# Transformer decode step on one core: output projection and second norm by token halves, sums of squares with tokens on partitions

## The reference

```
h    = rms_norm(x, norm_mix) * (1 + sc1) + sh1
q, k, v, u = split(h @ w_in)
attn = MoBA attention(q, k, v)       # sample: scores over all cached keys, top 3 blocks, cached values
pool = multi-scale pooling(u)
x    = x + g1 * (concat(attn, pool) @ w_out)             # output projection
h    = rms_norm(x, norm_mlp) * (1 + sc2) + sh2           # second norm
x    = x + g2 * (square(relu(h @ w_up)) @ w_down)        # MLP
y    = rms_norm(x, norm_final)
```

## Time and profile before

| | |
|---|---|
| runs (median, low, high) | 1012.74, 1011.08, 1019.36 us |
| profiled execution | 1017.83 us |
| its span, first to last instruction | 1014.6 us |
| TensorE busy | 912.3 us, 90% |
| VectorE busy | 538.7 us, 53% |
| ScalarE busy | 225.9 us, 22% |
| GpSimd busy | 150.2 us, 15% |
| granted TensorE clock, mean | 0.942 |

### The profile page before, as it was taken

The page is one execution under the profiler, slowest core; times in us unless marked ns, Lnnn a source line. Parts: engine busy times, 40 slices in busy tenths (PEclk is TensorE's granted clock), DMA queues, the critical chain, the costliest instruction groups (busy, mean ns, idle before and its releaser), DMA issues.

```text
span 1014.6 us, 16468 instructions
## 1 busy us (share of the span) xinstructions
PE 912.3 (90%) x6421; PEld 590.7 (58%) x6421; DVE 538.7 (53%) x936; ACT 225.9 (22%) x372; POOL 150.2 (15%) x150
## 2 busy tenths in 40 slices
PE   4939999999988997399989989999899999999896
PEld 3417777555544433266666657666666666676554
DVE  5374321478776375956647756756746422442124
ACT  3123220433321012112032131220220221313102
POOL 0040750000000000511011020120110110301100
PEclk9759999799999999599999999999999899999898
DMA  9710226778858787588788888888975977559992
GB/s 295 286 50 1 84 84 221 282 233 278 273 185 283 275 285 284 196 289 292 258 334 290 275 301 304 272 301 292 328 266 176 364 234 239 168 193 381 385 385 100
DMA packets 133183, 254.21 MB, mean 251 GB/s; under 512 B 10454, under 2 KB 61387, under 8 KB 124907
## 3 DMA queue, kind: packets, MB, share of 16 engines
q1 hardware_dynamic: 95475, 183.54, 51.6%
q10 hardware_dynamic: 36864, 67.13, 19.4%
q0 software_dynamic: 768, 2.51, 0.6%
HBM read 248.57 MB, written 4.75 MB: 250 GB/s over the span
## 4 chain that ended last, share of the span: by engine, by line
PE 68%; DVE 13%; DMA 8%; ACT 4%; ACTq 3%; issue 3%; POOL 1%; SPq 1%; DVEq 0%; POOLq 0%
PE PS L1407 65%; DVE KT L1043 4%; DMA W<-in_w_up_dram 3%; ACTq L805 3%; DMA VR<-in_w_up_dram 2%; DVE hT L987 1%; DVE hT L986 1%; ACT W_split L768 1%; DMA smp<-in_x_sample_dram 1%; PE PS L1582 1%; DVE W_split L1194 1%; DMA VR<-in_cache_v_dram 1%; PE PS L1421 1%; DMA KR<-in_cache_k_dram 1%; PE PS L1955 0%
## 5 line engine op out<-in xcount | busy, mean ns | idle before, releaser
L1407 PE MATMUL PS<-H_split,W_split 128*128 128x512 f32 x672 | 236.4, 414 | 14.9 <-DVE W_split L1016 14.9
L1407 PE MATMUL PS<-gT_split,W_split 128*128 128x512 f32 x512 | 172.8, 402 | 3.0 <-POOL kT_split L653 3.0
L1407 PEld LDWEIGHTS PS<-H_split,W_split 128*128 128x128 f32 x672 | 132.1, 197 | 68.2 <-issue 23.9
L1043 DVE STREAM_TRANSPOSE KT<-KR 128x512 f32<-128x512 f32 x256 | 161.5, 680 | 18.9 <-DMA KR<-in_cache_k_dram 18.9
L1407 PE MATMUL PS<-hT_split,W_split 128*128 128x512 f32 x320 | 129.8, 406 | 0.0
L1194 DVE TENSOR_TENSOR W_split<-W,W_split 128x1024 fp32r<-128x1024 f32 x64 | 82.0, 1285 | 86.8 <-ACT W_split L768 86.8
L1407 PEld LDWEIGHTS PS<-gT_split,W_split 128*128 128x128 f32 x512 | 96.1, 188 | 49.7 <-issue 18.7
L768 ACT ACTIVATE W_split<-W 128x1024 fp32r<-128x1024 f32 x64 | 67.2, 1051 | 237.6 <-DMA W<-in_w_up_dram 136.4
L1407 PE MATMUL PS<-KT,qcur 128*32 128x128 f32 (+1 forms) x2080 | 76.0, 288 | 38.8 <-DVE KT L1043 34.6
L1407 PE MATMUL PS<-kT_split,W_split 128*128 128x512 f32 x256 | 100.3, 392 | 0.0
L1407 PEld LDWEIGHTS PS<-KT,qcur 128*32 128x32 f32 x2080 | 54.8, 112 | 70.2 <-DVE KT L1043 49.0
(11 more groups left out here) (256 smaller groups left out, 987.9 us busy)
## 6 DMA issues: line engine op xcount, KB each, us to landing
KR<-in_cache_k_dram SPq DMA_DIRECT2D x256, 256.0 KB, 5.0
VR<-in_cache_v_dram ACTq DMA_DIRECT2D x256, 256.0 KB, 4.7
W<-in_w_up_dram SPq DMA_DIRECT2D x32, 512.0 KB, 7.1
W<-in_w_down_dram SPq DMA_DIRECT2D x32, 512.0 KB, 7.6
W<-in_w_in_dram SPq DMA_DIRECT2D x4, 2048.0 KB, 10.5
VR<-in_w_ada_dram SPq DMA_DIRECT2D x8, 1024.0 KB, 7.6
smp<-in_w_ada_dram SPq DMA_DIRECT2D x8, 1024.0 KB, 5.6
VR<-in_w_up_dram SPq DMA_DIRECT2D x3, 2048.0 KB, 10.3
```

The costliest lines, as they stand in the source:

```text
L1043: dve.transpose(ktb[:, t % 2, s, :], kring[:, t % 2, s, :]).then_inc(kt_ev, 1)
L1407: return pe.matmul(out, lhsT, rhs, start=start, stop=stop, **kw)
```

## The change

- The projection goes by token halves: 16 groups j (8 output tiles for tokens 0 to 255, then 8 for tokens 256 to 511) of 8 products of 256 columns, over 14 steps (8 to 21). H2_AT becomes 22; MLP_AT stays 24. `out_res(j)` now stands in the very step in which group j is finished (`groups_at`), ahead of `turn_unit`; the last one alone behind it. The copies of `rows` move ahead of it.
- The sum of squares is turned round: the squares are the weights and one column of ones moves, so the sum is 128 tokens on partitions by one column (2 products per group). Root and reciprocal are over 128x2. To bring it back to columns, VectorE multiplies it into the identity (128x256) and TensorE multiplies that by ones (`spread_root`).
- The norm of half 0 is made in steps 15 to 17 (4 tiles each in 16 and 17), of half 1 in step 22. A tile takes one VectorE instruction (`normal`), one on ScalarE that adds the shift and rounds (`second_high`), and one on VectorE (`low`), which was GpSimd's. In step 22 the turns of unit 23 stand between them.
- The first two MLP groups go by halves: group 0's half 0 at the head of step 23, the other three halves in step 24 and the first half of step 25.
- Parts 2 and 3 are loaded at step 18 and split at step 20, parts 4 and 5 loaded at step 22 and split in steps 24 and 25. A Sqrt on one column ahead of the last square brings ScalarE's table in early.

```diff
-        OUT_AT, H2_AT, MLP_AT = 8, 20, 24
+        OUT_AT, H2_AT, MLP_AT = 8, 22, 24
+        def groups_at(t):
+            return [j for j in range(OUT_GROUPS) if -(-(j + 1) * OUT_STEPS // OUT_GROUPS) - 1 == t - OUT_AT]
...
-                    sp.wait_ge(out_ps, 4 * (n // 2))
+                    sp.wait_ge(out_ps, FT + 4 * (n // 2))
...
-                if t == 14:
+                if t == 18:
                     load_part(2)
                     load_part(3)
-                if t == 20:
+                if t == 22:
                     load_part(4)
                     load_part(5)
...
-            stream_low(h2_high, h2_ready)
...
+            def root2(half):
+
+                act.wait_ge(ms2_ps, FT * half + FT)
+                act.activation(root[:, 2 * half:2 * half + 2], bank(0, P, 2, 2 * half), ACT.Sqrt, bias=eps[:, 0:1],
+                               scale=1.0 / D).then_inc(root2_done, 1)
+
+            def second_high(j):
+
+                f = j % FT
+                act.wait_ge(h2_raw, j + 1)
+                act.activation(h_hi[:, f, tokens(j)], hT[:, f, tokens(j)], ACT.Identity,
+                               bias=mods[:, SH2 + f, 0:1]).then_inc(h2_high, 1)
...
-                    if c:
-                        weights_high(8 * c + 3)
+                    weights_high(8 * c + 3 if c else 5)
...
+            def inverse_root(half):
+
+                dve.wait_ge(root2_done, half + 1)
+                link(dve.reciprocal(root[:, 2 * half:2 * half + 2], root[:, 2 * half:2 * half + 2]))
+                dve.tensor_tensor(rstd[:, half * HALF:half * HALF + HALF].rearrange("p (t n) -> p t n", t=2),
+                                  ident[:, None, :].to_broadcast([P, 2, P]),
+                                  root[:, 2 * half:2 * half + 2][:, :, None].to_broadcast([P, 2, P]), ALU.mult)\
+                   .then_inc(diag_done, 1)
...
-                if t in (10, 11, 13, 14, 16, 17, 19, 20):
-                    out_res((10, 11, 13, 14, 16, 17, 19, 20).index(t))
...
+                for j in groups_at(t):
+                    if j < OUT_GROUPS - 1:
+                        out_res(j)
+                if t in (16, 17):
+                    for j in range(4 * (t - 16), 4 * (t - 16) + 4):
+                        normal(j)
+                if t == H2_AT:
+                    for i in range(2):
+                        turn_keys(t + 1, i)
+                    inverse_root(1)
+                    normal(FT)
+                    normal(FT + 1)
+                    for j in range(FT, 2 * FT):
+                        low(j)
+                        if j + 2 < 2 * FT:
+                            normal(j + 2)
+                        if j in (FT + 3, FT + 5):
+                            turn_keys(t + 1, 2 + (j - FT) // 4)
                 else:
                     turn_unit(t + 1)
...
+            def mean_square(j):
+
+                m, half = j % FT, j // FT
+                pe.wait_ge(sq2_done, j + 1)
+                if j == FT:
+                    pe.wait_ge(root2_done, 1)
+                for i in range(2):
+                    lo = half * HALF + i * P
+                    last = mm(bank(0, P, 1, 2 * half + i), squares_mem[:, m % HP, lo:lo + P], ones[:, 0:1],
+                              m == 0 and i == 0, m == FT - 1, skip_group_check=True)
+                last.then_inc(ms2_ps, 1)
...
+            def spread_root(half):
+
+                pe.wait_ge(diag_done, half + 1)
+                pe.wait_ge(row_ev, ROWS)
+                mm(bank((1, 5)[half], P, HALF), ones[:, :], rstd[:, half * HALF:half * HALF + HALF]).then_inc(rstd_ps, 1)
...
+                if t == H2_AT + 1:
+                    up_half(0, 0)
                 sample_first(t)
```

More of the change, by code:

```diff
@@ L254, in decoder_step @@
         QBD = hT[:, 6:8, :].rearrange("p a (b h r) -> p (a b) h r", b=DB // 2, h=HP)
+        root = stat[:, 0:TT]
         rows_s = [hT[0:NS, 6, :], hT[0:NS, 7, :], scm[0:NS, 0:S]]
@@ L809, in _ @@
             act.wait_ge(page_in, 16)
-            for t in range(OUT_AT, H2_AT + 1):
+            for t in range(OUT_AT, MLP_AT):
                 b, x = softmax_of(t), t % 8
+                if t == H2_AT:
+                    root2(1)
                 if t >= LAG - 1:
@@ L840, in _ @@
                 if x == 0:
-                    if c:
-                        weights_high(8 * c + 2)
+                    weights_high(8 * c + 2 if c else 4)
                 if x == 1:
@@ L1324, in _ @@
                     turn_unit(t + 1)
-                    if c:
-                        weights_low(8 * c + 2)
+                    weights_low(8 * c + 2 if c else 4)
                 if x == 1:
@@ L1329, in _ @@
                         less_max(b)
-                    if c:
-                        weights_low(8 * c + 3)
+                    weights_low(8 * c + 3 if c else 5)
                     turn_unit(t + 1)
@@ new lines, in spread_root, with up_half @@
+            def spread_root(half):
+                pe.wait_ge(diag_done, half + 1)
+                pe.wait_ge(row_ev, ROWS)
+                mm(bank((1, 5)[half], P, HALF), ones[:, :], rstd[:, half * HALF:half * HALF + HALF]).then_inc(rstd_ps, 1)
+            def up_half(m, half):
+                cols = slice(half * HALF, half * HALF + HALF)
+                if half == 0:
+                    pe.wait_ge(part_low, m + 1)
+                for k in range(FT):
+                    if m == 0:
+                        pe.wait_ge(h2_ready, FT * half + k + 1)
+                    for term in range(3):
+                        ins = three_pass(bank(BANKS[m], P, HALF, half * HALF), up_view(part_hi(m))[:, k, :],
+                                         up_view(part_raw(m, W_split))[:, k, :], h_hi[:, k, cols], h_lo[:, k, cols],
+                                         term, k == 0, k == FT - 1)
+                if half:
+                    ins.then_inc(up_ps, 1)
@@ L1851, in mlp @@
                 c, x = (t - MLP_AT) // 8, t % 8
-                if x < 4:
+                if c == 0 and x < 2:
+                    if (x, half) != (1, 1):
+                        up_half(*((1, 0), (0, 1), (1, 1))[2 * x + half])
+                elif x < 4:
                     up(c, x, 12 * half, 12 * half + 12)
```

140 lines of the change are left out of this document (80 added, 60 removed).

## The result

The changed kernel takes 1036.32 us (median of 4 runs, 1032.55 to 1042.25), the kernel before in the same session 1014.64 (1011.08 to 1019.36): ratio 1.024, 95% interval 1.019 to 1.029. It is slower, by 21.7 us where 8.5 were forecast, and above the range (1001 to 1032). The profiled execution took 1033.14 with a span of 1031.3.

A forecast was written before the change was run, and what follows sets the result against it. It took TensorE, 90% busy, to be held in the gap before the MLP by a chain through VectorE. Terms 22.4 (A and B) - 21.1 - 2.3 + 4.4 + 1.7 + 3.4 = +8.5 on 1012.7 gave 1021.2 us, range 1001 to 1032.

The forecast's parts named there:

- G: Projection: TensorE's clock falls behind two of B's six waits of 2.5 to 3.65 us, +3.4 us (0 to 10.2).
- A: Projection: scores, values, heads and other work moved ahead of its end, +5.8 us.
- B: Projection, steps 8 to 19: TensorE waits for VectorE's turn behind the residual, 24.0 us, net +16.6.
- C: Gap between projection and MLP: shortened from 39.08 to 17.95 us, -21.1.
- D: First MLP groups by halves: a half-width fp32r product takes 0.13 us, -2.3 us after the gap.
- E: First chunk's second step: unit 26's turn waits for weight part 5's split in step 25, +4.4 us.
- F: Behind the wait of E: one fall of TensorE's clock, +1.7 us.
- R2: Slower rival, projection: every wait of B lets the clock fall, four more falls, +6.8, 1028.0 us; chance 0.2.
- R1: Faster rival, steps 9 to 19: the waits of B don't come, -11.5, 1001.2 us; chance 0.15.
- R4: Even-trade rival, projection: half of B is covered, 1012.9 us; chance 0.1.
- R3: Slower rival, MLP groups: half-width products cost as much as full ones, +5.5, 1026.7 us; chance 0.1.

The follow-up runs named there:

- e1: The changed kernel with VectorE's residual additions and first-half norm put behind the turn of the next unit; 1009.17 us, ratio 0.9948.
- e5: e1 with both first-half MLP groups early in step 23 and weight part 5's subtraction behind the turn of unit 26; 1003.04 us, ratio 0.9883.
- e6: e5 with the inverse root behind the scores' way out and weight parts 2 and 3 issued behind unit 20's keys; 994.54 us, ratio 0.9818.
- e4: The changed kernel with only weight part 5's low part moved behind the turn of unit 26; 1029.64 us, ratio 1.0152.
- e2: The changed kernel with products nobody reads added at the ends of steps 8, 9, 10, 14, 15, 16 and 17; 1015.2 us, ratio 1.0014.
- e8: The changed kernel with e2's filler products in steps 9, 14 and 16 alone; 1021.35 us, ratio 1.0119.
- e3: The kernel before, whole width, with row copies and residual ahead of the turn in the step where each group finishes; 1033.8 us, ratio 1.0172.
- e7: The changed kernel with the first two MLP groups on all tokens again; 1033.88 us, ratio 1.0192.
- e10: e6 with the first two MLP groups on all tokens again; 995.61 us, ratio 0.9836.
- e11: e6 with the turn of unit 26 put first in step 25 on VectorE; 995.96 us, ratio 0.9794.
- e12: e10 with the turn of unit 26 put first in step 25 on VectorE; 1001.57 us, ratio 0.984.

## Why the prediction was right and wrong

The mechanism of the gap and of the waits was right; the sum failed in its price for the clock, above all in term G. Term by term, from the profiles:

- **A**, work ahead of the projection's end: 5.8 forecast, 5.7 found (117.85 less 20.5 of clock is 97.4, before 91.6).
- **B**, the new waits: 24.0 forecast, 22.0 found, each at its step within 0.5 us; step 19's 1.4 didn't come. Net +14.6 for +16.6. e1 shows the cause by moving it: with the residual behind the turn the ratio falls by 0.029, the clock's share included.
- **C**, the gap: 17.95 forecast, 18.24 found; -20.8 for -21.1. It stays at 18.2 in e1, e5 and e6, since VectorE's list bounds it, not what TensorE does in it.
- **D**, half-width products: 0.13 forecast, 0.12 found. The Trainium skill ("TensorE: Matmul & The Clock Gate", Part 3) says that a weight load overlaps running products only when its row groups differ, which here would put load and columns in turn. The rows again disagree: a full load of weights and its 256 columns pass in 0.12 us, less than the 188 ns of one load in the earlier trace rows.
- **E**, step 26: 4.4 forecast, 4.62 found, taken away by e4.
- **F**, the fall behind it: 1.7 forecast, 3.4 found. The forecast also let both kernels start cold behind the gap; in the changed kernel no clock is missing there, in the kernel before 1.0 us is, so the change gained that 1.0.
- **G**, the falls in the projection: 3.4 forecast (0 to 10.2), 20.5 found. This is the step that failed.

G failed twice over. The count: "Of B's six waits of 2.5 to 3.65, I take two", because one of 2.55 in the kernel before had left the clock alone. Six falls came. One row without a fall was taken for a rule, where e4 and the changed kernel show the same wait of 2.11 with and without one, so that such a row is one draw. The trace of the kernel before held more rows than the one of 2.79: in chunks 1 to 4 the same scores wait 2.79, 2.55, 2.72 and 2.54 us, and a fall with 1.7 us missing follows each. The second of them, and stretches of 1 us behind it:

```profile
588.51 1.08 PE L1407 MATMUL PS<-KT,qcur 128*32 128x128 f32 x32 [2.55 <-DVE KT L1043]
```

```profile
589.00:590.00 1.00, 1.00 (x26) 0.87 1.07 399
590.00:591.00 1.00, 1.00 (x4) 0.50 1.02 399
```

So "the 2.55 that did nothing" stood beside another 2.55 that did. The price: "A fall costs 4 x 0.43 = 1.7", from the one fall that rows 8 show. That one was of the shortest kind, 3.4 us long; in the projection one lasted 3.4, four 6.8 and one 10.2, and TensorE worked through nearly all of it. Even the range's upper end for G, six falls at 1.7, was half of what came. With 20.5 for 3.4 and 3.4 for 1.7 the sum would be +27, and B's 2.0 less makes it +25; the profiles show +24.2.

e2 shows that it is the clock, and not something that came with the waits: the same instructions are held as long, TensorE is kept busy meanwhile, and 16.5 us of the projection are back. e8, with four waits bare, keeps four falls and 13.6 us.

Of the rivals, R2 (every wait lets the clock fall) had the mechanism right and its price at half, so that even its 1028.0 was too low. R1 and R4 fell with B's rows, R3 with D's. The sign mark set in the forecast, "five or more falls between 292 and 414, it is R2", was met: six.

What stays open is why a given wait of 1.5 to 3.3 us is followed by a fall or not. The Trainium skill ("TensorE: Matmul & The Clock Gate", Part 1) says that what sets the clock runs freely, without regard to the kernel's start, and varies from run to run. The traces agree as far as they go: identical waits in the changed kernel and e4 had different outcomes (2.11 no fall and fall; 3.08 with 1.7 and with 3.4 us missing). In e3, with the projection in whole groups, waits of 3.24 had none twice, while those of 4.64 and 2.45 had one each; whether its longer uninterrupted work between them matters wasn't tried.

## What to carry to other kernels

A wait on TensorE can have two prices, its length and the half-clock stretch behind it. Take the second from several falls in the trace and not from one: here it was mostly 3.4 us in the projection and mostly 1.7 in the MLP. And count every wait of the length in question in the whole trace: of the eight in the changed kernel's projection, 1.8 to 3.7 us long, all but one had a fall behind or between them. When an operation is pulled forward into the step in which its input comes ready, it blocks what stands behind it in its engine's list: put it behind what the bottleneck engine wants next (here five moves of a few lines, e1's, e5's two and e6's two, turned +2.4% into -1.8%). A gain from filling one wait is only kept if the next wait in line isn't set by another engine's chain, as e7 and e10 show in step 26.

## What the runs showed of the hardware

- The granted clock of TensorE fell behind waits as short as 2.11 us (e4), 1.83 (e2) and 1.53, and held through ones of 3.24 (e3). The shortest is in e6, where the clock is at 0.50 from 347.2 on, 2 us behind the wait:

```profile
345.18 0.40 PE L1477 MATMUL PS<-gsum,cst 128*128 128x16 f32 x2 [1.53 <-DVE tops L1159]
```

- In the projections the stretches at the lower level were between 3.4 and 10.2 us long and cost half their length.
- Products that nobody reads, in place of idling, gave back 2.3% of the kernel's time (e2 against the changed kernel, 1.0014 against 1.024).
- An fp32r product of 256 columns with its own load of 128 weights passes in 0.12 us, one of 512 columns in 0.244: half the width is half the time.
- Between executions of kernels with the same code there, the stage ahead of the projection differs by up to 9 us (start at 283.95 in e8, 293.00 in e5), and the long stretch from chunk 1 to the end by 6 (e6, e10, e11, e12). How much of the spread of the runs' times this is was not measured.
